# Prompt attention of a hybrid decoder step: values as the stationary operand, two heads in the two column halves of TensorE

## The reference, cut to what matters

```python
logits = einsum('btgrd,btkgd->btgrk', qg, ks) * (d ** -0.5)   # d = 64
logits = where(valid, logits, -inf)
p = softmax(logits, axis=-1)
o = einsum('btgrk,btkgd->btgrd', p, vs)                       # (tokens, 8 heads x 64)
```

## Time and profile before

| what | us |
|---|---|
| median of 3 runs | 2952.55 |
| lowest and highest of them | 2945.64, 2959.03 |
| profiled execution, its own time | 2948.62 |
| span of its instructions | 2946.9 |
| TensorE busy in the span | 2825.2 (96%) |
| VectorE busy | 1459.3 (50%) |
| ScalarE busy | 699.9 (24%) |
| GpSimd busy | 594.6 (20%) |

### The profile page before, as it was taken

How to read it: one execution, slowest core, us unless ns; L and a number is a source line. 1 busy time by engine, 2 the same in 40 slices (tenths; PEclk the granted TensorE clock), 3 DMA queues, 4 the chain that set the end, 5 groups by cost and what they waited for, 6 DMA issues and landing times. The chain is left out here.

```text
span 2946.9 us, 49899 instructions
## 1 busy us (share of the span) xinstructions
PE 2825.2 (96%) x19127; PEld 2744.1 (93%) x19127; DVE 1459.3 (50%) x3120; ACT 699.9 (24%) x1355; POOL 594.6 (20%) x376
## 2 busy tenths in 40 slices
PE   8999999999879987999989989989999999999998
PEld 7999999999879985999967979979999999999998
DVE  6223333322577747999914568657362233333233
ACT  5111111111333225131213455430231111111111
POOL 0112221122211002121222122122211122212210
PEclk9999999999989999999999999799999999999999
DMA  4111111111132221233354152235211111111101
GB/s 132 43 43 43 56 56 45 43 44 48 48 100 85 75 73 36 88 131 121 117 145 119 35 158 91 85 104 143 81 38 43 43 45 58 54 43 43 50 28 60
DMA packets 239559, 213.04 MB, mean 72 GB/s; under 512 B 27106, under 2 KB 216834, under 8 KB 239298
## 3 DMA queue, kind: packets, MB, share of 16 engines
q1 hardware_dynamic: 229122, 180.85, 20.6%
q10 hardware_dynamic: 6336, 18.88, 1.7%
q0 software_dynamic: 3968, 11.54, 1.5%
HBM read 168.00 MB, written 43.21 MB: 72 GB/s over the span
## 5 line engine op out<-in xcount | busy, mean ns | idle before, releaser
L592 DVE TENSOR_TENSOR ff_prod<-ff_silu,ff_gu 128x384 f32<-128x384 f32 x132 | 68.7, 520 | 798.7 <-ACT ff_silu L406 798.6
L97 PE MATMUL ff_gu<-front_hhi,ff_whi 128*128 128x384 f32 (+1 forms) x1056 | 340.7, 323 | 2.6 <-DVE front_hlo L536 2.3
L97 PE MATMUL ff_gu<-rear_hhi,rear_branches 128*128 128x384 f32 (+1 forms) x1056 | 338.6, 321 | 1.2 <-DVE rear_hlo L576 1.2
L99 PE MATMUL ff_gu<-front_hhi,ff_wlo 128*128 128x384 f32 (+1 forms) x1056 | 339.5, 321 | 0.0
L98 PE MATMUL ff_gu<-front_hlo,ff_whi 128*128 128x384 f32 (+1 forms) x1056 | 339.3, 321 | 0.0
L98 PE MATMUL ff_gu<-rear_hlo,rear_branches 128*128 128x384 f32 (+1 forms) x1056 | 338.5, 321 | 0.0
L99 PE MATMUL ff_gu<-rear_hhi,rear_branches 128*128 128x384 f32 (+1 forms) x1056 | 338.5, 321 | 0.0
L307 POOL TENSOR_TENSOR ff_wlo<-over_hand,ff_whi 128x1024 fp32r<-128x1024 f32 x62 | 149.2, 2428 | 582.6 <-ACT ff_whi L401 582.1
L406 ACT ACTIVATE ff_silu<-ff_gu 128x384 f32<-128x384 f32 x132 | 61.3, 465 | 858.5 <-PE ff_gu L99 858.4
L307 POOL TENSOR_TENSOR rear_branches<-ff_raw,rear_branches 128x1024 fp32r<-128x1024 f32 x62 | 149.7, 2434 | 571.0 <-ACT rear_branches L401 571.0
L97 PE MATMUL sel_proj<-front_hhi,proj_sel_whi 128*128 128x384 f32 (+1 forms) x672 | 215.5, 321 | 0.5 <-PEq L69 0.5
(11 more groups left out here) (403 smaller groups left out, 6692.4 us busy)
## 6 DMA issues: line engine op xcount, KB each, us to landing
scratch_feat<-sel_stage ACTq DMA_DIRECT2D x32, 528.0 KB, 2.7
proj_sel_raw<-in_w_in SPq DMA_DIRECT2D x28, 512.0 KB, 3.6
over_hand<-in_ffn_w_gate SPq DMA_DIRECT2D x22, 512.0 KB, 3.7
over_hand<-in_ffn_w_up SPq DMA_DIRECT2D x22, 512.0 KB, 3.7
over_hand<-in_ffn_w_down SPq DMA_DIRECT2D x22, 512.0 KB, 3.7
ff_raw<-in_ffn_w_down SPq DMA_DIRECT2D x22, 512.0 KB, 3.3
ff_raw<-in_ffn_w_gate SPq DMA_DIRECT2D x20, 512.0 KB, 3.9
ff_raw<-in_ffn_w_up SPq DMA_DIRECT2D x20, 512.0 KB, 3.8
```

What stands on the lines that cost most here:

```text
L97: nc.tensor.matmul(out, w_hi, x_hi, start=first, stop=False)
L99: return nc.tensor.matmul(out, w_lo, x_hi, start=False, stop=last)
L592: nc.vector.tensor_tensor(prod[:, 0:w], act_out[:, b, 0:w], gu[:, b, 1, 0:w], ALU.mult).then_inc(prod_done, 1)
```

## The change

The values become the stationary operand and the probabilities the moving one. For each pair of heads g = 0, 1 that differ in the value head, the product of one key tile is two matmuls: values 128 x 64 stationary, 128 columns of turned probabilities moving, the output in the lower or the upper 64 partitions of `out_ps`. The output so comes out with channels on the partitions and needs no turning. The products of a pair are spread over two steps: `mix_low` does the lower part of the key tiles of both heads in one step, `mix_high` the rest in the next. The order of heads in `steps` becomes 0, 2, 1, 3, 4, 6, 5, 7, and `probsT` gets four buffers. In TensorE's step a the order is now `score(a)`, `mix_low(a - 4)` or `mix_high(a - 5)`, `mix_pages`, `turn_probs(a - 2)`, `turn_share`.

The turned key tiles are shared out by halves: `low_tiles(t)` = (t + 2) // 2 go to VectorE, the rest to ScalarE. The custom instruction of VectorE scales by -SCALE and takes the minimum straight into `bias`, and the exponential has scale -1; TENSOR_SCALAR goes. The reciprocal row sums are spread by GpSimd to 128 x 512 (`share_wide`), turned by TensorE into `back_ps`, and VectorE multiplies `tile_out`, which ScalarE has copied from `out_ps`, in place. SyncE loads the queries one tile earlier.

```diff
-        probsT = s.sb("probsT", [P, 2, TILES, P])
+        probsT = s.sb("probsT", [P, 4, TILES, P])
...
-        steps = [(i, h) for i in range(TILES) for h in range(HEADS)]
+        steps = [(i, 4 * G + 2 * g + r) for i in range(TILES) for G in range(2) for r in range(2) for g in range(2)]
+        def low_tiles(t):
+            return (t + 2) // 2
... gpsimd
+            def spread_share(i):
+                pool.wait_ge(share_done, i + 1)
+                if i:
+                    pool.wait_ge(share_turned, i)
+                half = HEADS * HD // 2
+                for G in range(2):
+                    dst = share_wide[:, G * half:(G + 1) * half].rearrange("p (r g d) -> p r g d", r=2, g=2)
+                    src = share[:, 4 * G:4 * G + 4].rearrange("p (g r) -> p r g", g=2).unsqueeze(3)
+                    nc.gpsimd.tensor_copy(dst, src.broadcast_to([P, 2, 2, HD])).then_inc(share_spread, 1)
             for i in range(2, TILES):
                 split_q(i)
+                spread_share(i - 2)
+            spread_share(TILES - 2)
+            spread_share(TILES - 1)
... sync
+                if b == DB - 2:
+                    load_q(1)
-            load_q(1)
+            load_q(2)
             load_values(sp, range(SP_PAGES), pages_in)
             for i in range(2, TILES):
-                load_q(i)
+                if i + 1 < TILES:
+                    load_q(i + 1)
... tensor
+            def mix_low(a):
+                if a == 1:
+                    pe.wait_ge(loaded["v"], 16)
+                if a % HEADS == 1 and i:
+                    pe.wait_ge(heads_done, i)
+                pe.wait_ge(low_ready, a + 1)
+                last = mix_tiles(a, range(low_tiles(tile(i))))
+            def mix_high(a):
+                pe.wait_ge(high_ready, high_before(a + 1))
+                mix_tiles(a, range(low_tiles(t), t + 1)).then_inc(mixed, 1)
+            def mix_tiles(a, tiles):
+                n = a % HEADS // 2
+                for j in tiles:
+                    for g in range(2):
+                        last = nc.tensor.matmul(out_ps[g * HD:(g + 1) * HD, n * P:(n + 1) * P],
+                                                v[:, j, (2 * G + g) * HD:(2 * G + g + 1) * HD], probsT[:, (a - 1 + g) % 4, j, :],
+                                                start=(j == 0), stop=(j == t))
-                if 2 <= a <= len(steps) + 1:
-                    turn_probs(a - 2)
-                if 3 <= a <= len(steps) + 2:
-                    mix(a - 3)
+                if 5 <= a <= len(steps) + 3 and a % 2 == 1:
+                    mix_low(a - 4)
+                if 6 <= a <= len(steps) + 4 and a % 2 == 0 and tile(steps[a - 5][0]):
+                    mix_high(a - 5)
                 if 1 <= a <= LAST_SHARE:
...                     mix_pages
+                if 2 <= a <= len(steps) + 1:
+                    turn_probs(a - 2)
                 if a in out_steps:
-                    turn_out(out_steps.index(a))
+                    turn_share(out_steps.index(a))
... scalar
+                if a >= 12 and (a - 4) % HEADS == 0:
+                    act.wait_ge(mixed, PAIR * (i + 1))
+                    nc.scalar.activation(tile_out[:, i % 2, :, :], out_ps.rearrange("p (a b) -> p a b", b=P), ACT.Copy
+                                         ).then_inc(heads_done, 1)
-                if 2 <= a <= len(steps) + 1 and tile(steps[a - 2][0]) >= 4:
+                if 2 <= a <= len(steps) + 1 and tile(steps[a - 2][0]) >= 1:
... vector
-                nc.vector.tensor_tensor_reduce(logits[:, a % 2, 0:n], m, big[:, a % 2 * 1024:a % 2 * 1024 + n], 1.0,
-                                               FLOOR, ALU.add, ALU.max, top[:, a % 2:a % 2 + 1]).then_inc(masked, 1)
-                dve.wait_ge(masked, a + 1)
-                nc.vector.tensor_scalar(bias[:, a % 2:a % 2 + 1], top[:, a % 2:a % 2 + 1], -SCALE, None, ALU.mult
-                                        ).then_inc(bias_done, 1)
+                nc.vector.tensor_tensor_reduce(logits[:, a % 2, 0:n], m, big[:, a % 2 * 1024:a % 2 * 1024 + n], -SCALE,
+                                               -FLOOR, ALU.add, ALU.min, bias[:, a % 2:a % 2 + 1]).then_inc(masked, 1)
-                        nc.vector.tensor_tensor(dst, src, w.broadcast_to([P, 2, 2, HD]), ALU.mult).then_inc(heads_done, 1)
+                if a - 1 in out_steps:
+                    nc.vector.tensor_tensor(whole, whole, back_ps, ALU.mult).then_inc(out_kept, 1)
```

More of the change, by code:

```diff
@@ L1738, in attention @@
         share = s.sb("share", [P, HEADS])
-        heads = s.sb("heads", [P, HEADS * HD])
+        share_wide = s.sb("share_wide", [P, HEADS * HD])
         big = s.ps("big", [P, 6 * 512])
@@ L1777, in high_before @@
         def high_before(a):
-            return sum(1 for i, _ in steps[:a] if tile(i) >= 4)
+            return sum(1 for i, _ in steps[:a] if tile(i) >= 1)
         def load_pages(engine, cache, b, sems, which):
@@ L1973, in turn_probs @@
                 t = tile(steps[a][0])
+                m = low_tiles(t)
                 pe.wait_ge(exp_done, a + 1)
[L1975 to L1978, removed]
+                if a:
+                    pe.wait_ge(low_ready, a)
+                for j in range(m):
+                    last = nc.tensor.transpose(turned[:, 0, j * P:(j + 1) * P], probs[:, room(a), j * P:(j + 1) * P], ident[:, :])
@@ L1979, in turn_probs @@
+                last.then_inc(low_turned, 1)
+                if t:
+                    if a:
                         pe.wait_ge(high_ready, high_before(a))
-                    for j in range(4 * x, min(4 * x + 4, t + 1)):
-                        last = nc.tensor.transpose(turned[:, x, (j - 4 * x) * P:(j - 4 * x + 1) * P],
+                    for j in range(m, t + 1):
+                        last = nc.tensor.transpose(turned[:, 1, (j - m) * P:(j - m + 1) * P],
                                                    probs[:, room(a), j * P:(j + 1) * P], ident[:, :])
-                    last.then_inc((low_turned, high_turned)[x], 1)
@@ L1985, in mix @@
-            def mix(a):
+                    last.then_inc(high_turned, 1)
+            def mix_low(a):
                 i, h = steps[a]
-                t = tile(i)
-                if a == 0:
+                if a == 1:
                     pe.wait_ge(loaded["v"], 16)
-                if h == 0 and i:
-                    pe.wait_ge(heads_done, 2 * i)
+                if a % HEADS == 1 and i:
+                    pe.wait_ge(heads_done, i)
                 pe.wait_ge(low_ready, a + 1)
[L1993 to L1998, removed]
@@ L2000, in turn_out @@
-            def turn_out(i):
-                pe.wait_ge(heads_done, 2 * i + 2)
+                last = mix_tiles(a, range(low_tiles(tile(i))))
+                if tile(i) == 0:
+                    last.then_inc(mixed, 1)
+            def mix_high(a):
+                t = tile(steps[a][0])
+                pe.wait_ge(high_ready, high_before(a + 1))
+                mix_tiles(a, range(low_tiles(t), t + 1)).then_inc(mixed, 1)
+            def mix_tiles(a, tiles):
+                t = tile(steps[a][0])
+                n = a % HEADS // 2
+                G = n // 2
+                for j in tiles:
[3 more added lines that the diff above has]
+                                                start=(j == 0), stop=(j == t))
+                return last
@@ L2002, in turn_out, with turn_share @@
+            def turn_share(i):
+                pe.wait_ge(share_spread, 2 * i + 2)
                 if i:
@@ L2006, in turn_out @@
                 for n in range(4):
-                    last = nc.tensor.transpose(back_ps[:, n * P:(n + 1) * P], heads[:, n * P:(n + 1) * P], ident[:, :])
-                last.then_inc(out_turned, 1)
-            for a in range(len(steps) + 5):
+                    last = nc.tensor.transpose(back_ps[:, n * P:(n + 1) * P], share_wide[:, n * P:(n + 1) * P], ident[:, :])
+                last.then_inc(share_turned, 1)
+            for a in range(len(steps) + 6):
                 if 2 <= a < len(steps):
                     score(a)
-                if 2 <= a <= len(steps) + 1:
-                    turn_probs(a - 2)
-                if 3 <= a <= len(steps) + 2:
-                    mix(a - 3)
+                if 5 <= a <= len(steps) + 3 and a % 2 == 1:
+                    mix_low(a - 4)
+                if 6 <= a <= len(steps) + 4 and a % 2 == 0 and tile(steps[a - 5][0]):
+                    mix_high(a - 5)
                 if 1 <= a <= LAST_SHARE:
@@ L2098, in _ @@
             for G in range(2):
[L2099 to L2102 removed]
+                nc.vector.tensor_tensor_reduce(logits[:, G, :], masks[:, SLABS - 1, :], big[:, 1536 * G:1536 * G + SW], -SCALE,
+                                               -FLOOR, ALU.add, ALU.min, bias[:, G:G + 1]).then_inc(s_logits, 1)
             dve.wait_ge(loaded["own"], 16)
@@ L2139, in _ @@
                                   ).then_inc(new_kept, 1)
[L2140 to L2143 removed]
```

(5 more changed lines are left out.)

78 lines of the change are left out of this document (31 added, 47 removed).

## The result

The median over 7 runs is 2924.58 us (2918.28 to 2934.03) for the changed kernel and 2945.64 us (2937.96 to 2959.03) for the kernel before; the ratio is 0.992, with a 95% interval of 0.989 to 0.995. In a second set (8 and 14 runs) it was 2924.1 us against 2949.5, ratio 0.992 (0.990 to 0.995). The forecast was 2931 us, in a range of 2921 to 2943.

A forecast was written before the change was run, and what follows sets the result against it. TensorE bounds tiles 7 to 4, TensorE and VectorE both count in tiles 3 to 0. Terms -16.8 - 2.75 - 2.0 - 0.3 = -21.9 us, less 1.9 for waits, leave -20: forecast 2931 us, range 2921 to 2943.

The forecast's parts named there:

- The products: Prompt's 576 products with the values: 60 us before, 31.4 us after at 0.0545 us an instruction, a loss of 28.6 us.
- rival (A): Column halves do not work side by side when their moving data differ; products take 63 us, 2961 us in all; chance 6%.
- The change of form: TensorE going from full width to 64 columns and back: 0.25 us each, 48 times from step 17 on, 12 us.
- Rival (B): Going between full width and 64 columns costs 0.5 us, another 12 us, giving 2942 us; chance 12%.
- Tiles 6 to 4: Prompt windows where TensorE sets the pace: shorter products less the width changes give -5.75, -3.15 and -2.1 us.
- Tile 7: Prompt's steps 2 to 7: five heads of 1.68 us become three steps of 0.87 us, -5.8 us.
- Rival (D): TensorE's clock falls early, from tile 2 on; 8 to 16 us come back, giving 2942 us; chance 5%.
- Tiles 3 to 1: Late prompt windows, TensorE setting the pace: 15.0, 12.2, 9.9 us for 16.11, 13.25, 10.54, together -2.75 us.
- Rival (C): In tiles 3 to 0 the chain between engines stays the bound and windows keep their length: 2935 us; chance 15%.
- The end: From the last exponential's end to the stage's last copy: 4.47 us become 3.4, -1.1 us; with it tile 0 -2.0 us.
- turn and copy 0.7: First term after the last exponential: turning the last probabilities and copying them, taken as 0.7 us of the 3.4 us sum.
- Edits costed at nothing: Earlier query loads and the spreading queued behind GpSimd's query splitting, taken as free; the sample's two bias instructions go, -0.3 us.

## Why the prediction was right

- **The products**, -28.6 us: confirmed. From one start to the next they take 0.0545 us side by side (pairs every 0.109 us) and 0.109 in one half. The mechanism was read from a row of another stage with the same form, and rival (A) fell with it: twelve products take 0.81 us, where the run in one half, which does what (A) says, takes 1.45.
- **The change of form**, 0.25 us: measured 0.25 and 0.29. Rival (B) fell. The form is changed without waiting for the end of a whole instruction (0.27 us) on each side: from the last 64-column product to the first transpose are 0.20 us.
- **Tiles 6 to 4**, expected -5.75, -3.15, -2.1: measured -6.4, -3.5, -2.3. The old products cost a little more than 0.105 us each in the long runs.
- **Tile 7**, expected -5.8: -6.35 with the clock up, -0.7 and -3.5 in the two traces with a fall. Rival (D) had the mechanism in the wrong place: I looked at the small tiles, where the clock held until 1717.7 us, 3.3 us before the stage's end (1.8 in the kernel before). The thin steps are at the start, where the change took the products out of steps 3 and 4: scores, 8-column products and transposes, at 0.50 for 13.7 us. The Trainium skill (TensorE: Matmul & The Clock Gate, Part 4: PE-mode transpose) says that transposes don't count as TensorE's activity in the same way as other work. The trace agrees in that the clock stayed low over these steps, but no run here separates their three kinds of work, nor shows that the fall needs them.
- **Tiles 3 to 1**, expected -1.1, -1.05, -0.65: -1.8, -1.3, -1.0. TensorE waited for `tile_out` in four hand-overs, for 1.6 us in all and 0.5 at most; six or seven had been forecast, under 0.5 each. Rival (C) fell. But the reason given for the old lengths, VectorE's load, was half wrong: the halved copies alone made them longer.
- **The end**, expected -1.1 us and tile 0 -2.0: tile 0 lost 0.7. From the end of the last exponential (1716.48) to the last write (1720.98) are 4.5 us, as before. The step that failed is "turn and copy 0.7": the last two heads' turns and copies go one after the other and end at 1718.16, 1.7 us after the exponential. The four transposes took 1.12 us and not 0.7, since the clock had fallen by then, as it had before the change. The spreading was cheaper, 0.75 for 0.9. The forecast's own terms add up to 3.25 us, not the 3.4 it states.

```profile
1717.54 0.30 PE L2002 MATMUL att_turned<-core_ident,att_probs 128*128 128x128 f32 x1
1717.87 0.29 DVE L2191 COPY att_probsT<-att_turned 128x128 f32<-128x128 f32 x1 [0.48 <-PE att_turned L2002]
...
1718.34 0.75 POOL L1834 COPY att_share_wide<-att_share 128x256 f32<-128x256 f32 x2 [6.59 <-DVE att_share L2183]
...
1719.14 1.12 PE L2046 MATMUL att_big<-core_ident,att_share_wide 128*128 128x128 f32 x4 [0.22 <-POOL att_share_wide L1834]
```

- **Edits costed at nothing**: in the prompt's windows GpSimd's wait of 51.6 us for the query loads is gone and TensorE waited for no query. No run takes the earlier loads out alone.
- **The allowance** of 1.9 us for waits was not needed; the clock took its place. Without a fall the windows lost 23.0 us, where the sum before the allowance had 21.9 with the sample's 0.3. That the forecast of -20 us met a measured -21 (medians of the first set) is partly luck: the underestimate in tiles 7 to 1, the overestimate at the end and the fall that I had not seen offset each other. And the forecast time of 2931 us was made against a median of 2952.55, which became 2945.64 with more runs.

## What to carry to other kernels

A product with a narrow moving side can cost as much as one with a wide one: here 0.105 us with 64 moving columns and 0.109 with 128, on 128 x 128 weights. With the narrow operand stationary and two independent products in the two column halves the same work takes about half, at 0.25 to 0.3 us for each change of form, so put it beside work that has the form already. After a reordering, look at the clock column of the stage's thinnest steps, not only at its end: a fall there cost 3 to 6 us, and the two traces with a few idle products in the gaps before it had none. An edit that shifts work to an engine with time to spare can cost, if what it does there stands in the queue behind something long; try it in the schedule in which it will live.

## What was not expected of the hardware

TensorE starts matmuls of a free column half before earlier ones of the busy half: 8-column products began at 1627.26 us between 128-column ones that precede them in the program (1627.36, 1627.58). The Trainium skill (TensorE: Matmul & The Clock Gate, Part 3: Packing small matmuls) says that matmuls start and end strictly in program order. The measured starts differ from that, and so does the window of tile 6, which grew by 3.7 us where the run in one half grew by 6.7. And a whole stage that a change does not touch moved by 16 us between executions (the recurrence, 205.3 to 221.7), with its clock: 0.98 in the short ones, 0.90 to 0.93 in the longest.
